# Turning the attention weights by a product with a diagonal of inverse row sums, in a one-core float32 kernel

## The reference

```
s = einsum('bqhd,bkhd->bhqk', q, k) * scale + bias_or_mask      # -inf where a key is not seen
prob = softmax(s, -1)                                            # exp(s - max) / sum
out  = einsum('bhqk,bkhd->bqhd', prob, v)
```

## Time and profile before

| | us |
|---|---|
| time before, median of 3 runs | 3868.04 |
| lowest and highest of the 3 | 3867.3 and 3870.64 |
| the profiled execution, its own time | 3864.45 |
| span of its trace | 3862.7 |
| first sparse stage in the trace | 69.2 |
| second sparse stage | 69.2 |
| band stage | 136.4 |

### The profile page before, as it was taken

The page is one execution under the profiler, slowest core; times in us unless marked ns, Lnnn a source line. Parts: engine busy times, 40 slices in busy tenths (PEclk is TensorE's granted clock), DMA queues, the critical chain, the costliest instruction groups (busy, mean ns, idle before and its releaser), DMA issues. The chain is left out here.

```text
span 3862.7 us, 43362 instructions
## 1 busy us (share of the span) xinstructions
PE 3343.2 (87%) x16972; PEld 2709.8 (70%) x16972; DVE 2297.0 (59%) x3573; ACT 1318.6 (34%) x1866; POOL 630.8 (16%) x548
## 2 busy tenths in 40 slices
PE   8976778997996787998994888879999897699998
PEld 7763567886872566886763876767778787577787
DVE  7868646995658645996645663554442433644534
ACT  2123524772122623774312111123232324632222
POOL 0025501000006501000502341301100102511000
PEclk8986788999996787999996997889999998899999
DMA  7620004991530002992220000002222221022222
GB/s 277 239 88 0 1 17 158 375 375 72 207 120 0 1 20 84 374 375 114 87 82 11 1 1 1 1 12 104 77 94 93 86 90 48 28 93 87 88 98 77
DMA packets 59578, 401.33 MB, mean 104 GB/s; under 512 B 6768, under 2 KB 8432, under 8 KB 12272
## 3 DMA queue, kind: packets, MB, share of 16 engines
q1 hardware_dynamic: 53616, 356.62, 25.0%
q0 software_dynamic: 5760, 41.95, 3.0%
HBM read 396.45 MB, written 2.10 MB: 103 GB/s over the span
## 5 line engine op out<-in xcount | busy, mean ns | idle before, releaser
L135 PE MATMUL ps<-t_part,weight_hi 128*128 128x512 f32 x2152 | 863.4, 401 | 69.9 <-DVE scr_part L180 38.4
L137 PE MATMUL ps<-t_part,ring_lo 128*128 128x512 f32 x2152 | 851.4, 396 | 0.0
L136 PE MATMUL ps<-scr_part,weight_hi 128*128 128x512 f32 x1640 | 650.4, 397 | 0.0
L347 DVE TENSOR_TENSOR ring_lo<-ring,weight_hi 128x2048 fp32r<-128x2048 f32 x133 | 311.1, 2339 | 386.7 <-ACT weight_hi L340 386.7
L135 PEld LDWEIGHTS ps<-t_part,weight_hi 128*128 128x128 f32 x2152 | 413.5, 192 | 163.6 <-DVE ring_lo L167 69.7
L340 ACT CAST weight_hi<-ring 128x2048 fp32r<-128x2048 f32 x133 | 253.7, 1907 | 667.6 <-PE ps L137 667.6
L137 PEld LDWEIGHTS ps<-t_part,ring_lo 128*128 128x128 f32 x2152 | 412.0, 191 | 87.9
L136 PEld LDWEIGHTS ps<-scr_part,weight_hi 128*128 128x128 f32 x1640 | 316.9, 193 | 69.2 <-issue 3.9
L136 PE MATMUL ps<-big_part,weight_hi 128*128 128x512 f32 x512 | 200.3, 391 | 0.0
L201 POOL TENSOR_TENSOR big<-big 128x512 f32<-128x512 f32 x28 | 47.9, 1709 | 891.7 <-ACT big L194 888.2
L449 DVE SCALAR_TENSOR_TENSOR scr_q<-t,c_act,scr_q 128x256 f32<-128x256 f32 x294 | 142.6, 485 | 10.5
(11 more groups left out here) (613 smaller groups left out, 7222.9 us busy)
## 6 DMA issues: line engine op xcount, KB each, us to landing
ring<-in_w_moe SPq DMA_DIRECT2D x84, 1024.0 KB, 5.1
t<-in_w_moe SPq DMA_DIRECT2D x84, 1024.0 KB, 4.9
ring<-in_w SPq DMA_DIRECT2D x64, 1024.0 KB, 4.8
t<-in_w_ada POOLq DMA_DIRECT2D x40, 1024.0 KB, 5.2
ring<-in_w_in SPq DMA_DIRECT2D x32, 1024.0 KB, 5.9
ring<-in_even_in SPq DMA_DIRECT2D x15, 1024.0 KB, 4.8
ring<-in_qkv SPq DMA_DIRECT2D x12, 1024.0 KB, 4.8
ring<-in_w_out SPq DMA_DIRECT2D x8, 1024.0 KB, 4.8
```

The lines of the kernel that those rows point to most:

```text
L135: pe.matmul(bank, w_hi, x_hi, start=first, stop=False)
L136: pe.matmul(bank, w_hi, x_lo, start=False, stop=False)
L137: return pe.matmul(bank, w_lo, x_hi, start=False, stop=last)
L347: v.tensor_tensor(K.ring_lo[:, g % NSLOT, :], K.ring[:, g % NSLOT, :], K.w_hi[:, n % 2, :].bitcast(F32), ALU.subtract).then_inc(w_lo.up(), 1)
```

## The change

Items are no longer normalised before they are turned. POOL instead multiplies the 128x128 identity by the item's column of reciprocals, which gives a diagonal matrix, and PE turns each block by a real product of the block with that diagonal: the result is the block transposed with each column already divided by its row's sum. Four diagonals are held in turn, so that POOL waits for turn(n - 4) before it writes the one for n. The steps for the lo parts of keys and queries on POOL are moved: keys after the diagonal of (H,2), queries after that of (H,3). ACT rounds the keys of a pair after exp(H,1), where before it did so after exp(H,3), right ahead of the queries. `scores(h, 0)` now waits for the keys' lo part first and for the queries' lo part only before its third product.

```diff
         def scores(n):
             if t == 0:
-                pe.wait_ge(ql.sem, ql.at(prepared(h)))
+                pe.wait_ge(qh.sem, qh.at(prepared(h)))
+                pe.wait_ge(ql.sem, ql.at(prepared(h) - 1))
...
             pe.matmul(bank(n)[:, 0:w], q_hi, k(h // 2)[1][:, 0:w], start=False, stop=False)
+            if t == 0:
+                pe.wait_ge(ql.sem, ql.at(prepared(h)))
             pe.matmul(bank(n)[:, 0:w], q_lo, k_hi(h // 2)[:, 0:w], start=False, stop=True).then_inc(sc.up(), 1)
         def turn(n):
-            pe.wait_ge(no.sem, no.at(n + 1))
+            pe.wait_ge(di.sem, di.at(n + 1))
...
             for b in range(t + 1):
-                ins = pe.transpose(turned(n, S)[:, b * P:(b + 1) * P], p(n)[:, b * P:(b + 1) * P], K.ident[:, :])
+                ins = pe.matmul(turned(n, S)[:, b * P:(b + 1) * P], p(n)[:, b * P:(b + 1) * P], diagonal(n),
+                                start=True, stop=True)
# POOL
         for n in range(N):
             g.wait_ge(rs.sem, rs.at(n + 1))
-            w = (items[n][1] + 1) * P
-            g.tensor_tensor(p(n)[:, 0:w], p(n)[:, 0:w], col(n, 3).to_broadcast([P, w]), ALU.mult).then_inc(no.up(), 1)
+            if n >= 4:
+                g.wait_ge(tr.sem, tr.at(n - 3))
+            g.tensor_tensor(diagonal(n), K.ident[:, :], col(n, 3).to_broadcast([P, P]), ALU.mult).then_inc(di.up(), 1)
             if n < ST:
                 values_lo(n)
-            if n % ST == 1 and n // ST + 2 < heads:
-                operands_lo(n // ST + 2)
+            if n % ST == 2 and n // ST % 2 == 0 and n // ST + 2 < heads:
+                keys_lo(n // ST + 2)
+            if n % ST == 3 and n // ST + 2 < heads:
+                queries_lo(n // ST + 2)
# ACT
                 exponentials(n)
                 if n == 0:
-                    operands_hi(1)
+                    queries_hi(1)
+                if n % ST == 1 and n // ST % 2 == 0 and n // ST + 2 < heads:
+                    keys_hi(n // ST + 2)
                 if n % ST == 3 and n // ST + 2 < heads:
-                    operands_hi(n // ST + 2)
+                    queries_hi(n // ST + 2)
```

More of the change, by code:

```diff
@@ L968, in softmax_attention @@
 def softmax_attention(K, name, heads, q, k, v_raw, v_parts, scale, bias, out, tiles, k_hi, more_p, bias_source=None):
-    sc, ma, ex, no = K.sig("score_product"), K.sig("masked"), K.sig("exponentials"), K.sig("normalised")
+    sc, ma, ex, di = K.sig("score_product"), K.sig("masked"), K.sig("exponentials"), K.sig("normalised")
     tr, ph, pl_, pv, oe = (K.sig(n) for n in ("probs_turned", "probs_hi", "probs_lo", "head_product", "head_summed"))
@@ L984, in softmax_attention @@
         "p (b q) -> p b q", b=ST)
+    diagonals = [K.scr_p[:, :], K.scr_p2[:, :], K.T1[:, 3840:3968], K.T1[:, 3968:4096]]
+    diagonal = lambda n: diagonals[n % 4]
     turned = lambda n, w: K.ps[:, (2, 3, 7)[n % 3], 0:w]
@@ L1048, in values_lo, with keys_lo, queries_lo @@
             g.tensor_tensor(lo, raw, hi.bitcast(F32), ALU.subtract).then_inc(vl.up(), 1)
[L1050 to L1059, removed]
+        def keys_lo(h):
+            g.wait_ge(qh.sem, qh.at(prepared(h) - 1))
+            g.tensor_tensor(k(h // 2)[1], k(h // 2)[0], k_hi(h // 2).bitcast(F32), ALU.subtract).then_inc(ql.up(), 1)
+        def queries_lo(h):
+            g.wait_ge(qh.sem, qh.at(prepared(h)))
+            g.wait_ge(ql.sem, ql.at(prepared(h) - 1))
+            g.wait_ge(di.sem, di.n)
+            g.tensor_tensor(q_part(h, 1)[rows(h), :], q(h), q_part(h, 0)[rows(h), :].bitcast(F32),
+                            ALU.subtract).then_inc(ql.up(), 1)
+            g.wait_ge(ql.sem, ql.at(prepared(h)))
         for n in range(N):
             g.wait_ge(rs.sem, rs.at(n + 1))
-            w = (items[n][1] + 1) * P
-            g.tensor_tensor(p(n)[:, 0:w], p(n)[:, 0:w], col(n, 3).to_broadcast([P, w]), ALU.mult).then_inc(no.up(), 1)
+            if n >= 4:
+                g.wait_ge(tr.sem, tr.at(n - 3))
+            g.tensor_tensor(diagonal(n), K.ident[:, :], col(n, 3).to_broadcast([P, P]), ALU.mult).then_inc(di.up(), 1)
             if n < ST:
                 values_lo(n)
-            if n % ST == 1 and n // ST + 2 < heads:
-                operands_lo(n // ST + 2)
+            if n % ST == 2 and n // ST % 2 == 0 and n // ST + 2 < heads:
+                keys_lo(n // ST + 2)
+            if n % ST == 3 and n // ST + 2 < heads:
+                queries_lo(n // ST + 2)
     def v_(v):
@@ L1125, in s_, with keys_hi, queries_hi @@
     def s_(s):
-        def operands_hi(h):
+        def keys_hi(h):
+            s.copy(k_hi(h // 2), k(h // 2)[0]).then_inc(qh.up(), 1)
+        def queries_hi(h):
             if h >= 2:
                 s.wait_ge(sc.sem, sc.at(ST * (h - 1)))
-            if h % 2 == 0:
-                s.copy(k_hi(h // 2), k(h // 2)[0]).then_inc(qh.up(), 1)
             s.copy(q_part(h, 0)[rows(h), :], q(h)).then_inc(qh.up(), 1)
@@ L1152, in probs_hi @@
             s.copy(pt(h, 0)[:, 0:t + 1, t * P:w], turned(n, w).rearrange("p (b q) -> p b q", q=P)).then_inc(ph.up(), 1)
-        operands_hi(0)
+        keys_hi(0)
+        queries_hi(0)
         for n in range(N + 7):
```

## The result

The changed kernel takes 3835.14 us (median of four runs, 3828.75 to 3837.99) against 3869.34 for the kernel before in the same session: ratio 0.9909, 95% interval 0.9892 to 0.9926. That is 34.2 us less, where the forecast was 35.0 less and 3833. The profiled execution took 3832.49 us with a span of 3830.7, 32.0 less than the earlier trace rows.

The account below looks back on a forecast made before the run. Bound: a chain of waits through ACT, POOL's operand parts, normalisation of (H,2) and PE's turn. Gains of 12.3 (both sparse stages), 20.1 (band) and 2.6 (openings), together 35 us, took 3868.0 to 3833; range 3819 to 3850.

Parts of the forecast that it names:

- What bounds the kernel: Three stages: POOL makes operand parts before normalising (H,2), so PE idles 2.56 us in a long interval.
- The chain after: PE, ACT and DVE between head products: 5.50 plus 0.33 for the product, 5.83 us, taken as 6.0.
- The 5.50 interval: Earlier trace, first sparse stage: interval with no operand parts on POOL, taken as the chain that stays.
- PE's load: PE's busy time a head: 4.76 us plus 1.1 for ten more blocks, 5.9, tying with the chain.
- The product: PE's turn: a block costs 0.22 us where it cost 0.11, so (H,2) is rounded 0.33 later.
- The last interval and the keys: Last interval of a stage 4.65 us; ACT's keys rounding covered in sparse stages, up to 0.25 late in band.
- The opening: Start of each stage to first head product: net gains +1, +1 and +0.6, 2.6 us together.
- the clock's part: Openings: about 0.5 us lost to the low clock after PE's new wait for queries_lo(2).
- (a): POOL's queries_lo or ACT's key rounding late after all, every interval 6.57 us: 3848 us, chance 0.14.
- (d): Another wait, such as PSUM's three turned banks, stands where POOL's wait was: 3868 us, chance 0.04.
- (b): The products hide entirely, chain at 5.50 us: 49 us less, 3819 us, chance 0.06.
- (c): PE becomes the bound in the turns, 0.44 us a block and 8.1 a head: 3893 us, chance 0.06.

Follow-up runs that it names:

- e1: Changed kernel with the new order alone, items still normalised on POOL and transposed on PE: 3829.8 us, ratio to before 0.9895.
- e2: Kernel before with the diagonals and the product alone, order of parts untouched: 3872.0 us, ratio to before 1.0009.
- e3: Changed kernel, diagonals made and waited for, but blocks turned by transposes and the division left out: 3829.0 us, ratio to before 0.9899.
- e4: Changed kernel with ACT's move(H-2) put behind its rounding of item (H-1,3): 3823.7 us, ratio to before 0.9887.

## Why the prediction was right

*What bounds the kernel.* Right. That POOL's order held (H,2) back was read from the earlier trace rows, and e1 and e2 show it from both sides: the order without the product gains 41.4 us, the product without the order 0.9.

*The chain after.* The forecast chain was 5.83; measured 5.86, with each step within 0.05 of its place (rounding +2.78 for +2.76, widest item +4.50 for +4.47). The 5.50 interval without operand parts in the earlier trace rows was the right pattern. I took 6.0 since PE's load tied with the chain; for the steady state that margin was 0.14 too large, 3.6 us over 26 intervals. That the sum of the 26 came out all the same, 155.5 us for 156, is luck: the first intervals of two stages, partly at the low clock, took 1.7 and 1.1 us more (7.54 and 6.93), and the keys' rounding 0.7.

*The product.* 640 records in the place of 320, and 17292 PE products on the page for 16972. For a diagonal kept in scr_p:

```profile
L1026 PE MATMUL ps<-scr_p,t x156: 272/275/583, 359.5 to 3330.7; 128*128 128x128 f32 x156
```

Median 275 ns, where the earlier trace rows has 274 as the least; on the chain 0.35 for 0.33 (e3). The Trainium skill's factor of four ("TensorE: Matmul & The Clock Gate", Terms) is not what a turn of one block costs here: two records of 0.11 us for one, a factor of two.

*The last interval and the keys.* 4.73 for 4.65; the keys' rounding 0.11 late in the band stage where up to 0.25 was allowed.

*The opening.* This is the term that was mis-sized. To the first head product, from the start of the stage on ACT, it is 17.5 us for 19.2 in the first sparse stage, 16.6 for 19.3 in the second and 22.2 for 23.3 in the band stage: 1.7, 2.8 and 1.1, or 5.5 in all, where +1, +1 and +0.6 were forecast. The 1.6 of the forecast before the clock's part is too small: the second stage, where the clock did not fall again before the head product, gained 2.8. The clock's part isn't 0.5 a stage either, but all or nothing. The first interval is 7.54 us in the first sparse stage and 5.83 in the second, in the same execution. A normal interval and the start of the slow one:

```profile
382.80:388.70 5.90, 5.69 (x40) 5.28 (x40) 4.66 (x19) 5.64 (x16) 3.67 (x6) 1.00 0.01 3
...
369.00:372.50 3.50, 3.50 (x14) 3.31 (x14) 0.93 (x4) 1.53 (x6) 1.39 (x2) 0.50 0.00 0
```

The clock fell while PE idled for 1.14 us at the queries' part, until 367.05, and at 0.50 (1.2 GHz) the eight head products take 2.59 us and not 1.49. In the second stage PE idled for 1.13 us at the same place, and its clock stayed high.

*The sum.* Forecast 35.0 from the stages. Measured from ACT's first rounding it is 38.2: 32.7 in the intervals between head products, where 32.4 were forecast, and 5.5 in the openings for 2.6. By stage it is 6.9 and 9.8 for 7.15 each with the opening, and 21.5 for 20.7. By the spans it is 32.0, since the rest of the program, untouched, took 3598.6 us in the trace before and 3604.8 in the changed one, and the 34.2 of the medians lies between. That it came within 1 us of the forecast is in part luck.

*Rivals.* (a), intervals of 6.57, and (d), another wait in the same place, are refuted by the intervals of 5.86. (b), the products hide, is refuted by e3. (c), PE as the bound in the turns at 8.1 us, fell with a block at two records and intervals of 5.86; that PE's own load doesn't hold the 5.86 either is shown by e4, though PE is busy for 96% of the stretch above.

## What to carry to other kernels

When a chain of waits shows one engine idle behind another, look at what stands in front of the awaited instruction in the other engine's queue, not at how busy that engine is: here a move of two steps was worth 41 us, and a step shorter by 0.43 us at the same place took 0.43 off a wait of 2.56, most of which the dearer product then spent. An interval in the same trace in which the suspected work is absent (the last heads) forecasts the kernel without that wait: 5.50 there, 5.51 in e1. A change with two parts should be timed in parts: the second part of this one took back some 5 us of what the first gave.

## What the runs showed of the hardware

A float32 product of 128x128 costs PE two records of 0.11 us at 2.4 GHz, a transpose of the same block one. The granted clock was 1.00 over 64 us in which 110 of PE's 333 records were such transposes (e1), and over the 3.86 us of 32 transposes in a row in the kernel before (from 2502.87). Whether the clock is low in the first interval of a stage differs between two stages of one execution with the same instructions (7.54 and 5.83 us), which is worth 1.7 us; what decides it isn't shown here. And the rest of the program, untouched, varied by 14 us between executions, more than the difference between the changed kernel and most of the experiments.
